# Two transformer blocks on one core: the stick-breaking values beside the fox values, a reordered latent chain, reordered mixer ends, and the conv stream 80 columns further on

## The reference

```python
u = _rmsnorm(h, mix_pre_g[l]); proj = u @ w_in[l]
q_sb, k_sb, v_sb, q_fx, k_fx, v_fx, f_logit, q_mem = jnp.split(proj, split_at, axis=-1)
w = jnp.where(mask, jnp.exp(log_beta + log_between), 0.0)      # stick-breaking: o_sb = w @ v_sb
c = lax.cumsum(log_sigmoid(f_logit + b_forget), axis=2)        # fox: softmax(q.k + c_q - c_k) @ v_fx
merged = (g_sb * (_merge_heads(o_sb) @ w_br_sb[l]) + g_fx * (_merge_heads(o_fx) @ w_br_fox[l])
          + g_mem * (_merge_heads(o_mem) @ w_br_mem[l]))
h = h + _rmsnorm(merged @ w_out[l], mix_post_g[l])
# second block
ckv = rms_norm(h, kv_in_norm) @ w_dkv                          # 256 latent + 64 rope columns
kv = rms_norm(c_kv, kv_norm) @ w_ukv                           # k_nope, v of 8 heads
q = rms_norm(x_n @ w_dq, q_norm) @ w_uq                        # 8 heads x (128 + 64)
g, u = jnp.split(causal_dwconv(x_n @ w_up, conv_w), 2, axis=-1)  # conv feed-forward
```

## Time and profile before

| | |
|---|---|
| median of 3 runs | 1869.18 us (1869.04 to 1869.72) |
| the profiled execution | 1869.25 us, of which the span is 1867.4 us |
| PE busy | 1843.3 us, 99% of the span |
| DVE, ACT busy | 1210.5 us (65%), 1035.3 us (55%) |
| POOL busy | 98.8 us (5%) |
| DMA | 333.83 MB, mean 179 GB/s |

### The profile page before, as it was taken

One profiled execution on the slowest core, in us unless ns is written; L12 is line 12 of the kernel. 1 busy time (PEld: TensorE's weight loads), 2 busy tenths in 40 slices (PEclk: granted clock), 3 DMA queues, 4 the chain that ended last, 5 costly groups with the idle time before them and its releaser, 6 DMA issues.

```text
span 1867.4 us, 26977 instructions
## 1 busy us (share of the span) xinstructions
PE 1843.3 (99%) x10455; PEld 1623.2 (87%) x10455; DVE 1210.5 (65%) x1824; ACT 1035.3 (55%) x1680; POOL 98.8 (5%) x78
## 2 busy tenths in 40 slices
PE   8999999999999999999999999999999999899998
PEld 6888899998888888888999888888889998879997
DVE  5555657677765466545777776555768765758763
ACT  6545544556554455445555655445557655757653
POOL 0000001110000000000011100000002210001210
PEclk9999999999999999999999999999999999999999
DMA  7655575445576547654654547654757654637662
GB/s 259 218 181 180 160 206 166 139 147 184 164 226 186 191 150 229 189 188 139 187 175 139 186 144 234 181 191 148 213 148 215 186 190 131 190 102 203 191 194 102
DMA packets 353792, 333.83 MB, mean 179 GB/s; under 512 B 25338, under 2 KB 299392, under 8 KB 353664
## 3 DMA queue, kind: packets, MB, share of 16 engines
q1 hardware_dynamic: 353120, 331.58, 57.9%
q10 hardware_dynamic: 544, 0.52, 0.1%
HBM read 330.97 MB, written 1.05 MB: 178 GB/s over the span
## 4 chain that ended last, share of the span: by engine, by line
PE 90%; DVE 5%; ACT 2%; DMA 1%; issue 1%; SPq 0%; ACTq 0%; DVEq 0%
PE bank L1680 21%; PE bank L1682 21%; PE bank L1681 21%; PE bank L1691 7%; PE bank L1693 7%; PE bank L1692 7%; PE bank L1697 3%; DVE wlo L1072 2%; DMA raw<-in_w_in 1%; ACT whi L553 1%; DVE ulo L1120 1%; DVE bank L1363 0%; PE bank L1932 0%; ACT uhi L579 0%; PE bank L1971 0%
## 5 line engine op out<-in xcount | busy, mean ns | idle before, releaser
L1072 DVE TENSOR_TENSOR wlo<-raw,whi 128x1024 fp32r<-128x1024 f32 (+3 forms) x638 | 761.4, 1202 | 447.0 <-ACT whi L553 444.2
L553 ACT ACTIVATE whi<-raw 128x1024 fp32r<-128x1024 f32 (+3 forms) x638 | 648.3, 1025 | 498.4 <-PE bank L1682 403.3
L1680 PE MATMUL bank<-whi,uhi 128*128 128x512 f32 (+2 forms) x1232 | 471.7, 383 | 3.0 <-DVE wlo L1072 2.0
L1682 PE MATMUL bank<-wlo,uhi 128*128 128x512 f32 (+2 forms) x1232 | 459.9, 373 | 0.0
L1681 PE MATMUL bank<-whi,ulo 128*128 128x512 f32 (+2 forms) x1232 | 459.2, 373 | 0.0
L1691 PE MATMUL bank<-uhi,whi 128*128 128x256 f32 x1024 | 293.1, 286 | 0.2 <-DVE gates L1261 0.2
L1692 PE MATMUL bank<-ulo,whi 128*128 128x256 f32 x1024 | 289.7, 283 | 0.0
L1693 PE MATMUL bank<-uhi,wlo 128*128 128x256 f32 x1024 | 289.6, 283 | 0.0
L1680 PEld LDWEIGHTS bank<-whi,uhi 128*128 128x128 f32 x1232 | 231.7, 188 | 37.8 <-DVE wlo L1072 3.4
L1682 PEld LDWEIGHTS bank<-wlo,uhi 128*128 128x128 f32 x1232 | 231.4, 188 | 35.4
L1681 PEld LDWEIGHTS bank<-whi,ulo 128*128 128x128 f32 x1232 | 231.8, 188 | 32.8
(11 more groups left out here) (287 smaller groups left out, 1725.7 us busy)
## 6 DMA issues: line engine op xcount, KB each, us to landing
raw<-in_ffn_w_up SPq DMA_DIRECT2D x351, 256.0 KB, 3.6
raw<-in_ffn_w_down SPq DMA_DIRECT2D x264, 256.0 KB, 2.9
raw<-in_ffn_w_gate SPq DMA_DIRECT2D x175, 256.0 KB, 3.0
raw<-in_w_gate SPq DMA_DIRECT2D x128, 192.0 KB, 3.0
raw<-in_w_in SPq DMA_DIRECT2D x80, 256.0 KB, 3.4
raw<-in_a_w_in SPq DMA_DIRECT2D x48, 256.0 KB, 3.3
raw<-in_w_mem_kv SPq DMA_DIRECT2D x32, 256.0 KB, 3.4
raw<-in_w_out SPq DMA_DIRECT2D x32, 256.0 KB, 2.9
```

Of the source, the lines that this page charges most:

```text
L553: act.activation(whi[n % SLOTS][:, 0:w], raw[n % RAW][:, 0:w], ACT.Copy).then_inc(hi_ready, 1)
L1072: dve.tensor_tensor(wlo[n % SLOTS][:, 0:w], raw[n % RAW][:, 0:w], whi[n % SLOTS][:, 0:w].bitcast(F32), ALU.subtract).then_inc(lo_ready, 1)
L1680: pe.matmul(dst, xh, wh, start=start, stop=False)
L1682: return pe.matmul(dst, xh, wl, start=False, stop=stop)
```

## The change

It changes the order of the instructions on PE, ACT and DVE at several places, the engine that issues one transfer, and the address of two buffers. No product is added or dropped; one busy transpose count changes from 6 + 8 to 12 + 4 + 6. The unused buffer `line` shrinks by 80 columns, so what lies behind it stays at its addresses. In the token-block product of the conv stages `uhi, ulo` likewise become `conv_hi, conv_lo`, as in the hunk at 2144. `c_mem` is the stage of the memory's values, `c_v[1]` the first stage of the second layer's mixer.

```diff
@@ -121,7 +121,12 @@
 H = sb("H", [P, TT, DM])
-uhi, ulo = sb("uhi", [P, KT, TOK], F32R), sb("ulo", [P, KT, TOK], F32R)
+U = sb("U", [P, 2 * KT * TOK + 80], F32R)
+ucols = lambda at: U[:, at:at + KT * TOK].rearrange("p (k n) -> p k n", k=KT)
+uhi, ulo = ucols(0), ucols(KT * TOK)
+conv_hi, conv_lo = ucols(80), ucols(KT * TOK + 80)
+stream_hi = lambda b: conv_hi if b in (7, 9) else uhi
+stream_lo = lambda b: conv_lo if b in (7, 9) else ulo
@@ -400,7 +405,6 @@
     sp.dma_start(H[:, 0, :], A["x"][0, ts[0], :]).then_inc(x_loaded[0], 16)
-    sp.dma_start(param_rows[0:2 * KT, 0, :], A["ffn1_pre_g"].rearrange("l (k p) -> (l k) p", p=P)).then_inc(pre_loaded, 16)
@@ -537,6 +541,7 @@
 def _(act):
+    act.dma_start(param_rows[0:2 * KT, 0, :], A["ffn1_pre_g"].rearrange("l (k p) -> (l k) p", p=P)).then_inc(pre_loaded, 16)
@@ -576,7 +581,7 @@
             src = bank[acc(b) + 2 * t + nb][:, (k % 4) * P:(k % 4 + 1) * P]
-            act.activation(uhi[:, k, ts[t]], src, ACT.Copy, scale=par[:, g:g + 1]).then_inc(uhi_done, 1)
+            act.activation(stream_hi(b)[:, k, ts[t]], src, ACT.Copy, scale=par[:, g:g + 1]).then_inc(uhi_done, 1)
@@ -652,7 +657,7 @@
         post_root(b, 1)
-        if n0 == c_v[1]:
+        if n0 in (c_v[1], c_mem):
             split_to(n0 + 5)
@@ -783,10 +788,9 @@
+    split_to(0)
+    act.wait_ge(par_ready, 1)
     for t in range(TT):
-        act.wait_ge(par_ready, 1)
-        if t == 0:
-            split_to(0)
         u_high(0, t, 0)
         if t == 0:
@@ -922,11 +926,14 @@
     h_squares(b, 0)
-    both_high(1)
+    for nb in range(2):
+        u_high(b, 1, nb)
     h_squares(b, 1)
     for t in range(TT):
         h_root(b, t)
-    split_to(c_kv + 3)
+    for nb in range(2):
+        act.wait_ge(u_done, 16 * b + 8 + 4 * nb + 4)
+        kv_high(1, nb)
@@ -943,11 +950,11 @@
     latent_root(0, 0, QL)
-    split_to(c_uqr)
+    split_to(c_kv + 3)
     act.wait_ge(w_used, c_dq + 4)
     latent_square(0, 1, bank[5][:, :], stat(8, 1, RSTD))
     latent_root(0, 1, QL)
-    split_to(c_hp)
+    split_to(c_uqr + 1)
     act.wait_ge(lt_full, 1)
@@ -1024,10 +1031,10 @@
     mla_exp(2)
+    take_key(2)
     mla_exp(3)
+    take_value(2)
     heads(0, mla_pT)
-    take_key(2)
-    take_value(2)
     split_to(c_hp + 5 + SLOTS)
@@ -1117,7 +1124,7 @@
             src = bank[acc(b) + 2 * t + nb][:, (k % 4) * P:(k % 4 + 1) * P]
-            dve.scalar_tensor_tensor(ulo[:, k, ts[t]], src, par[:, g:g + 1], uhi[:, k, ts[t]].bitcast(F32),
+            dve.scalar_tensor_tensor(stream_lo(b)[:, k, ts[t]], src, par[:, g:g + 1], stream_hi(b)[:, k, ts[t]].bitcast(F32),
@@ -1186,11 +1193,9 @@
         post_norm(b, 1)
-        if n0 == c_v[1]:
-            split_to(n0 + 4)
+        if n0 in (c_v[1], c_mem):
+            split_to(n0 + 5)
         u_low(b, 1, 0)
-        if n0 == c_v[1]:
-            split_to(n0 + 5)
         u_low(b, 1, 1)
@@ -1372,7 +1377,6 @@
-        split_to(n0 + 7 + SLOTS)
@@ -1393,13 +1397,15 @@
         last_branch(0)
+        split_to(w0 + 1)
+        merged_low(0, 0)
         split_to(w0 + 2)
-        merged_low(0, 0)
         merged_low(0, 1)
         split_to(w0 + 3)
         last_branch(1)
+        split_to(w0 + 4)
+        merged_low(1, 0)
         split_to(w0 + 5)
-        merged_low(1, 0)
@@ -1408,6 +1414,7 @@
     u_low(0, 0, 0)
+    split_to(1)
     u_low(0, 0, 1)
@@ -1536,20 +1543,18 @@
     residual(b, 1, lambda nb: wait_f(b, 1, nb))
+    split_to(n0 + 5)
     for nb in range(2):
         dve.wait_ge(vhi_done, 4 * nb + 4)
         kv_low(0, nb)
-    for nb in range(2):
         u_low(b, 1, nb)
-    split_to(n0 + 5)
-    h_bias(b, 0)
+    for t in range(TT):
+        h_bias(b, t)
+    for t in range(TT):
+        h_rstd(b, t)
     for nb in range(2):
         dve.wait_ge(vhi_done, 8 + 4 * nb + 4)
         kv_low(1, nb)
-    h_bias(b, 1)
-    for t in range(TT):
-        h_rstd(b, t)
-    split_to(c_kv + 3)
@@ -1599,11 +1604,11 @@
-    turn_query(0)
     for k in range(2):
         dve.wait_ge(lat_hi, 6)
         dve.scalar_tensor_tensor(llo[:, 12 + k, :], bank[2][:, k * TOK:(k + 1) * TOK], par[:, KVN + k:KVN + k + 1],
                                  lhi[:, 12 + k, :].bitcast(F32), ALU.mult, ALU.subtract).then_inc(lat_lo, 1)
+    turn_query(0)
@@ -1643,8 +1648,8 @@
     heads(2, mla_max)
+    heads(2, mla_norm)
     split_to(c_hp + 7 + SLOTS)
-    heads(2, mla_norm)
     heads(1, mla_low)
@@ -1913,7 +1918,7 @@
             pe.wait_ge(m_taken, 6 * LAYERS)
-        for h in range(3):
+        for h in range(MH):
@@ -1924,7 +1929,6 @@
         pe.matmul(bank[3][0:8, 64 + P:64 + TOK], flog[:, 0, :], ones, start=False, stop=True).then_inc(c_full, 1)
-        mem_query(3)
@@ -1964,8 +1968,6 @@
             feature_chunk(0)
-            if p > 0:
-                sb_out(p - 1)
             pe.wait_ge(q_taken, l * MH + MH)
@@ -2029,6 +2031,7 @@
             gate_chunk(1, 2)
             gate_chunk(1, 3)
+            sb_out(p)
             pe.wait_ge(fx_pt, I * 2 + 2)
@@ -2052,8 +2055,6 @@
                 ins.then_inc(w_used, 1)
-                if i == 0 and k == 1:
-                    sb_out(3)
@@ -2080,18 +2081,18 @@
-    pe.wait_ge(cst_loaded, 16)
-    pe.wait_ge(pre_loaded, 16)
-    pe.transpose(bank[0][:, 0:2 * KT], param_rows[0:2 * KT, 0, :], ident[0:2 * KT, 0:2 * KT]).then_inc(par_tp, 1)
-
     def keep_busy(n):
         for i in range(n):
             turn(ident, bank[1][:, (i % 4) * P:(i % 4 + 1) * P])
-    keep_busy(6)
+    pe.wait_ge(cst_loaded, 16)
+    keep_busy(12)
+    pe.wait_ge(pre_loaded, 16)
+    pe.transpose(bank[0][:, 0:2 * KT], param_rows[0:2 * KT, 0, :], ident[0:2 * KT, 0:2 * KT]).then_inc(par_tp, 1)
+    keep_busy(4)
     for nb in range(2):
         stream_turn(0, 0, nb)
-    keep_busy(8)
+    keep_busy(6)
     pe.wait_ge(par_ready, 1)
@@ -2144,7 +2145,7 @@
                 start_chunk(n)
-                project(bank[conv_bank(f)][:, s * TOK:(s + 1) * TOK], n, KT, uhi, ulo).then_inc(w_used, 1)
+                project(bank[conv_bank(f)][:, s * TOK:(s + 1) * TOK], n, KT, conv_hi, conv_lo).then_inc(w_used, 1)
@@ -2179,14 +2180,13 @@
-    latent_keys(0)
-    latent_keys(1)
+    for j in range(3):
+        latent_keys(j)
     pe.wait_ge(lat_done, 2)
     for k in range(4):
         for t in range(TT):
             ins = turn(qtok[:, t, k * P:(k + 1) * P], bank[k // 2][:, (k % 2) * TOK + t * P:(k % 2) * TOK + (t + 1) * P])
     ins.then_inc(lt_full, 1)
-    latent_keys(2)
     latent_keys(3)
     qh, ql, kvh, kvl = lhi[:, QLAT, :], llo[:, QLAT, :], lhi[:, KVLAT, :], llo[:, KVLAT, :]
```

4 lines of the change are left out of this document (2 added, 2 removed).

## The result

The changed kernel takes 1853.65 us (median of 4 runs, 1853.23 to 1853.9), the kernel before 1869.13 us (1869.04 to 1869.72): a ratio of 0.9916, 95% interval 0.9904 to 0.9927, 15.5 us faster. The prediction was 1857.4 us with a range from 1853.5 to 1862 us; by the ratio (0.9916 x 1869.18 = 1853.48 us) the result stands at the range's lower edge, just outside it. About 4 us more came than the sum had.

What follows compares the result with a forecast made beforehand. The prediction took PE, with 90% of the chain of waits, to bound the kernel. Its terms, 2.05 + 0.9 + 2.1 + 0.65 + 2.1 + 0.75 + 3.2 = 11.75 us, gave 1857.4 us, range 1853.5 to 1862 us.

Steps and rivals of the forecast that it cites:

- What bounds the kernel: Whole kernel: PE holds 90% of the chain; a change counts only where PE stands still or pays for a change of form.
- The buffers 80 columns on: Conv stages' stream at another address: nothing gained or lost, since 811 matmuls in 97 us show no gap to fill.
- a sign of being wrong: Wrong if the 811 matmuls in 97 us move, or new PE idle in latent chain and heads exceeds 3 us.
- a rival with the right sign: Conv stream's new address is fast: 5 to 10% a matmul, 12 to 24 us gained, 1845 to 1833 us; chance 0.03.
- The slow rival: Conv stream's new address is read more slowly: at 10% a matmul the kernel takes 1881 us; chance 0.02.
- Start: Kernel start: rows issued first by ACT, twelve early transposes, one wlo moved between the halves: 2.05 us, bounds 1.3 and 2.7.
- c_mem and the forget gate's wait: PE's wait for wlo in c_mem goes, 0.9 us; memory query ahead of the cumulative sum covers layer 1's flog wait, 0.65 us.
- c_v[1]: Layer 2's first mixer stage: PE's wait for a wlo goes, as it now precedes a low part: 0.75 us, bounds 0.5 and 0.75.
- Values beside the fox values: Mixer pairs: stick-breaking values moved next to the fox values, 0.26 us a pair, 2.1 us over 8 pairs.
- Mixer ends: PE's waits for M and ulo at both mixers' ends shrink: 1.05 us a layer, 2.1 us in two; bounds 1.2 and 2.5.
- Latent chain and heads: Stalls at qtok and in the heads: 1.3 us at the queries' turn, 1.9 us in the heads; 3.2 us, bounds 1.5 and 5.0.
- the waits form again: DVE, ACT and chunk landing bind at start, latent part and mixer ends: 4.35 us taken back, 1861.8 us; chance 0.12.

Runs made afterwards that it cites:

- the scan: Three kernels, each the kernel after with another offset of the stream in each stage (8 to 128 columns): 1860.66, 1854.9 and 1854.12 us, one run each.

## Why the prediction was right and wrong

*What bounds the kernel.* Right that PE sets the time, wrong that a change counts only where PE stands still or changes its form. PE's pace without any wait was not a constant.

*The buffers 80 columns on.* This is the step that failed: "nothing", because the count of matmuls showed no gap. The runs show 4.0 to 4.2 us in 1920 matmuls, 120.0 ns against 117.8 ns. By the prediction's own words this is a sign of being wrong, since the count went from 811 to 826. I had a rival with the right sign, but gave it a chance of 0.03 and argued against it that "the matmuls of other streams at other addresses stand at the same 0.12 us". That was no evidence: all those streams lay whole multiples of 512 bytes from the weights, and the scan shows that 128 columns, which are 512 bytes, act like 0. So none of the trace's rows could have shown another pace. (The slow rival even says that nothing in the trace shows a stream at another address.) The size was also off: 1.8% of a matmul's distance, under the 5 to 10% that I had assumed.

*Start.* The order of the steps was right, the size wrong: 2.05 us were forecast, 1.46 to 1.55 us came. Idle time before chunk 1, which should have gone, is still 0.19 us. The step was that the first chunk "is now rounded ahead of the wait for par, in time that ACT spends waiting", with 0.5 us for the extra issue. The chunk landed at 7.5 us and not at 6.4, since it came behind the rows not by the time of their issue but by more; ACT's conversion then stood on the path. The Trainium skill (DMA: Bandwidth & Descriptors, "Issuing engines are not separate DMA queues") says that issuing on several engines at once saves only the sequencer's time for the issue; that would be 0.93 us for the rows (0.73 against 1.66 us). The rows landed 3.4 us sooner: first in ACT's queue they took 1.9 us from the issue, third in SP's 4.4 us, third in ACT's 5.2 us. The other 2.5 us are those of standing ahead of the large transfers. This doesn't refute the rule, since no run issues the rows first from SP.

*c_mem and the forget gate's wait.* Right: 0.99 for 0.92 us, 0.73 for 0.65 us.

*c_v[1].* Wrong: 0.75 us forecast, 0.00 came. The wait for the chunk did go; the next thing that DVE owed was rb, behind two conversions that wait for ACT. I had not asked what is late next, though I did so at the start and at the merged stream. The run with rb first, 1.04 us, shows that this wait took its place.

*Values beside the fox values.* Right in its mechanism, 2.7 us for 2.1 us, 0.29 us a middle pair for 0.26 us (0.16 to 0.20 us in the first pair of a layer); the small four cost 0.22 us inside a run of narrow matmuls. The last pair of a layer, in the branch product, gave more, 0.45 and 0.48 us, and so did one pair in layer 0, 0.63 us, where PE had also waited for a chunk.

*Mixer ends.* Right: 1.3 us a layer for 1.05 us. The second wait went whole, where I had left 0.2 us.

*Latent chain and heads.* The sum was right, 2.9 us for 3.2 us, its two terms less so. The stall at `qtok` is gone, new ones stand at `ctk` (1.74 + 0.16 us) and `qra` (1.07 + 0.16 us), and a third of 0.71 + 0.16 us in the heads. That is 4.0 us of new idle time, over the 3 us that the prediction names as a sign of being wrong; the gain is there because 6.8 us of idle time, counted alike, went. From the first turn of H behind the conv stage, the queries' turn comes 0.46 us sooner (38.73 against 39.19 us) where 1.3 us were forecast, with a lower bound of 0.5 us, and the heads gain 2.5 us (55.79 against 58.26 us) for 1.9 us. That the two errors nearly cancel is luck. The first term also varies: in other kernels with the same latent code the queries' turn stands at 37.7 to 39.1 us, with 0.7 to 2.2 us of wait at `ctk`, and what sets that wait was not found. The heads take 55.8 to 56.0 us in all of them. The experiments did not take this part alone, so its division into steps is read from the profiles and not shown by a run of its own.

*The rivals.* That the waits form again came true at c_v[1] and in part at the start, for 1.3 us together. With the conv stream at column 0 the kernel takes 1857.87 us, so the sum of all other terms, 11.75 us, was off by 0.4 us. That it came so close is luck in part: the start and c_v[1] gave 1.3 us less, the values and the mixer ends 1.1 us more.

What stays open: what decides which of its two paces a stretch takes, and why 0, 64 and 128 columns have only the slow one of 120.0 ns. The distance between stream and weights bears on the pace; what stood ahead of the stretch and the phase in which it begins may decide the rest, and no run varied them alone. That the two operands are read from the same banks at the same time would fit, and was not shown. It was not tried to move the stationary stream and the weights against each other for the products of 512 columns beyond the places listed.
